# First norm of a two-layer block: turned by chunks of two feature tiles, gain applied as columns, and another order of the first fetches

## What is computed

```python
h = rmsnorm(x, g_mix[l])                 # x * rsqrt(mean(x*x) + eps) * gain, per token
dq, dk, dv, c_q, c_kv_kr, xq, gate_logits = jnp.split(h @ w_in[l], split_idx, axis=-1)
cos_d, sin_d = rotary_tables(positions, DIFF_HEAD_DIM)   # cos, sin of position * inv_freq
cos_r, sin_r = rotary_tables(positions, MLA_ROPE_DIM)
```

## Time and profile before

| | |
|---|---|
| median of 3 runs | 3456.38 us (3451.1 to 3456.73) |
| profiled execution | 3450.06 us |
| its span, first to last instruction | 3448.8 us |
| TensorE (PE) busy | 3329.5 us, 97% |
| VectorE (DVE) busy | 2017.9 us, 59% |
| ScalarE (ACT) busy | 1313.8 us, 38% |
| granted TensorE clock, mean | 0.992 |

### The profile page before, as it was taken

The page is one execution under the profiler, slowest core; times in us unless marked ns, Lnnn a source line. Parts: engine busy times, 40 slices in busy tenths (PEclk is TensorE's granted clock), DMA queues, the critical chain, the costliest instruction groups (busy, mean ns, idle before and its releaser), DMA issues.

```text
span 3448.8 us, 52979 instructions
## 1 busy us (share of the span) xinstructions
PE 3329.5 (97%) x21876; PEld 2720.4 (79%) x21876; DVE 2017.9 (59%) x3798; ACT 1313.8 (38%) x2468; POOL 0.2 (0%) x4
## 2 busy tenths in 40 slices
PE   7989999999999999999999999999999999999998
PEld 6777788888888777788888888777677788788887
DVE  6776753554447776743544448775766578564434
ACT  5466543342225465543332224222443224132222
POOL 0000000000000000000000000000000000000000
PEclk9999999999999999999999999999999999999999
DMA  4221223233333221223333324223311334333332
GB/s 141 80 69 50 56 80 104 86 104 98 98 101 118 90 77 38 59 76 110 98 92 98 98 98 123 81 90 112 114 40 31 108 83 153 122 99 98 98 98 86
DMA packets 353767, 315.11 MB, mean 91 GB/s; under 512 B 10276, under 2 KB 281764, under 8 KB 353528
## 3 DMA queue, kind: packets, MB, share of 16 engines
q1 hardware_dynamic: 352808, 309.56, 29.7%
q10 hardware_dynamic: 720, 2.16, 0.2%
HBM read 288.09 MB, written 23.59 MB: 90 GB/s over the span
## 4 chain that ended last, share of the span: by engine, by line
PE 81%; DVE 11%; ACT 4%; issue 3%; DMA 1%; SPq 0%; DVEq 0%; ACTq 0%
PE banks L532 14%; PE banks L534 13%; PE banks L533 13%; PE banks L427 8%; PE banks L429 8%; PE banks L428 8%; DVE weights_r L368 2%; PE banks L632 1%; PE banks L2877 1%; PE banks L2816 1%; ACT weights_high_r L361 1%; PE banks L1228 1%; PE banks L1241 1%; PE banks L1332 1%; PE banks L2574 1%
## 5 line engine op out<-in xcount | busy, mean ns | idle before, releaser
L368 DVE TENSOR_TENSOR weights_r<-weights,weights_high_r 128x1024 fp32r<-128x1024 f32 (+2 forms) x517 | 593.3, 1155 | 345.8 <-ACT weights_high_r L361 344.7
L532 PE MATMUL banks<-h_T_hi,weights_high_r 128*128 128x512 f32 (+2 forms) x1912 | 760.0, 397 | 9.6 <-DVE h_T_lo L881 3.8
L534 PE MATMUL banks<-h_T_hi,weights_r 128*128 128x512 f32 (+2 forms) x1912 | 737.7, 386 | 0.0
L533 PE MATMUL banks<-h_T_lo,weights_high_r 128*128 128x512 f32 (+2 forms) x1912 | 736.8, 385 | 0.0
L361 ACT ACTIVATE weights_high_r<-weights 128x1024 fp32r<-128x1024 f32 (+2 forms) x517 | 510.6, 998 | 352.0 <-DMA weights<-in_w_mlp 214.0
L532 PEld LDWEIGHTS banks<-h_T_hi,weights_high_r 128*128 128x128 f32 x1912 | 360.8, 189 | 100.3 <-issue 31.4
L534 PEld LDWEIGHTS banks<-h_T_hi,weights_r 128*128 128x128 f32 x1912 | 360.6, 189 | 72.4
L533 PEld LDWEIGHTS banks<-h_T_lo,weights_high_r 128*128 128x128 f32 x1912 | 361.2, 189 | 68.5 <-issue 3.6
L427 PE MATMUL banks<-weights_high_r,h_T_hi 128*128 128x512 f32 (+2 forms) x672 | 278.2, 414 | 3.9 <-DVE weights_r L368 2.1
L429 PE MATMUL banks<-weights_high_r,h_T_lo 128*128 128x512 f32 (+2 forms) x672 | 253.7, 378 | 0.0
L428 PE MATMUL banks<-weights_r,h_T_hi 128*128 128x512 f32 (+2 forms) x672 | 253.3, 377 | 0.0
(11 more groups left out here) (555 smaller groups left out, 5205.6 us busy)
## 6 DMA issues: line engine op xcount, KB each, us to landing
weights<-in_w_in SPq DMA_DIRECT2D x183, 512.0 KB, 3.8
weights<-in_w_mlp SPq DMA_DIRECT2D x128, 512.0 KB, 3.8
weights<-in_ffn_w_in SPq DMA_DIRECT2D x44, 512.0 KB, 3.8
weights<-in_w_out SPq DMA_DIRECT2D x24, 512.0 KB, 3.6
weights<-in_ffn_w_down SPq DMA_DIRECT2D x22, 512.0 KB, 3.6
weights<-in_w_mem_kv SPq DMA_DIRECT2D x16, 512.0 KB, 3.6
weights<-in_w_diff_o SPq DMA_DIRECT2D x16, 512.0 KB, 3.6
weights<-in_w_mla_o SPq DMA_DIRECT2D x8, 512.0 KB, 3.4
```

Source lines behind the costliest of these rows:

```text
L368: ve.e.tensor_tensor(self.part(c.w_raw_r, u), self.part(c.w_raw, u), self.part(c.w_high_r, u).bitcast(F32), ALU.subtract).then_inc(*ve.tel ...
L532: pe.e.matmul(out, lhsT=wh[:, k, :], rhs=hi[k][:, cols], start=(k == 0), stop=False)
L533: pe.e.matmul(out, lhsT=wh[:, k, :], rhs=lo[k][:, cols], start=False, stop=False)
L534: mm = pe.e.matmul(out, lhsT=wl[:, k, :], rhs=hi[k][:, cols], start=False, stop=(k == self.chunks - 1))
```

## The change

StartNorm is rewritten in eight steps. The gain comes as eight columns (one per feature tile) in one small array with the identity, and is applied behind the turning: as the scale of ScalarE's high copy and as the scalar of VectorE's low part. What is turned is x times the inverse root alone (`dve_scale` for tiles 0 and 2, `act_scale` for 1 and 3). A bank now holds two feature tiles of a pair of token tiles (`pe_turn(pair, b)`), each part is made by two instructions of 256 columns, and cq's unit u waits only for chunk b = u (`chunk_ready`). Chunks stand between cq's steps in all three engines' orders, with lags on TensorE for the second pair. The multiplications by g_mix and its fetch are gone from layer 0. On SyncE's queue identity with gain is first, then the six units of weights without a wait for x, then positions and inverse frequencies, vectors and mem. The squares wait for x alone and no longer for the identity. The whole of the tables' VectorE work is now at 7.8 and 7.9, behind all eight chunks' low parts (the last is at 7.7); the sines stay at 11.6. `x_gone` is now: tile 3 squared and tiles 2 and 3 scaled.

```diff
@@ -412,6 +413,8 @@
             part = wh.shape[1]
             if first:
                 pe.wait_ge("low", u)
+                for k in range(part):
+                    pe.wait_all(self.chunk_ready(n, k0[u] + k))
                 if callable(self.ready):
                     for k in range(part):
...
 
-    def tile_scaled(self, t, g, lane):
-        self.c.values[("scaled", self.tag, t, g)] = lane.end
-
     def sp(self):
-        sp = self.c.sp
-        sp.wait_ge("x_in", 1)
         self.c.stream.sp(0)
         for _ in range(self.n):
             yield
 
-    def pe_turn(self, t):
+    def cols(self, pair):
+        return slice(2 * pair * P, 2 * (pair + 1) * P)
+
+    def got(self, pair, b, k):
+        return self.c.slots[(self.tag, pair, b)][:, k * 2 * P:(k + 1) * 2 * P]
+
+    def pe_turn(self, pair, b):
         c, pe = self.c, self.c.pe
-        for g in range(2):
-            pe.wait_ge("scaled", self.tag, t, g)
-            bank = c.fill(self.tag, t, g, ring=self.ring)
-            for k in range(4):
-                at = (4 * g + k) * P
-                mm = pe.e.transpose(bank[:, k * P:(k + 1) * P], self.xg[:, t, at:at + P], c.ident[:, :])
-            mm.then_inc(*pe.tell("filled", self.tag, t, g))
+        for t in (2 * pair, 2 * pair + 1):
+            pe.wait_ge("scaled", self.tag, t, b // 2)
+        bank = c.fill(self.tag, pair, b, ring=self.ring)
+        for k in range(2):
+            at = (2 * b + k) * P
+            for t in range(2):
+                mm = pe.e.transpose(bank[:, (2 * k + t) * P:(2 * k + t + 1) * P], self.xg[:, 2 * pair + t, at:at + P], c.ident[:, :])
+        mm.then_inc(*pe.tell("filled", self.tag, pair, b))
 
     def pe(self):
-        for pair in ((), (), (0, 1), (), (2,), (3,)):
-            for t in pair:
-                self.pe_turn(t)
-            yield
+        self.c.pe.wait_ge("in", "identity")
+        for pair in range(2):
+            for b in range(4):
+                self.pe_turn(pair, b)
+                yield
 
     def act_squares(self, t):
...
         c, ac = self.c, self.c.ac
+        ac.wait_ge("inverse_root", self.roots[t - 1].tag)
         for g in range(2):
-            ac.wait_ge("filled", self.tag, t, g)
-            ac.wait_all(self.free)
-            ac.e.activation(self.tile(c.hT_all[0], t, g), self.got(t, g), ACT.Copy).then_inc(*ac.tell("turned_high", self.tag, t, g))
+            ac.e.activation(self.halves(self.xg[:, t, :])[g], self.halves(c.x[:, t, :])[g], ACT.Copy,
+                            scale=self.sums[0][:, t:t + 1]).then_inc(*ac.tell("scaled_act", self.tag, t, g))
+            c.values[("scaled", self.tag, t, g)] = ac.end
+
+    def act_high(self, pair, b):
+        c, ac = self.c, self.c.ac
+        ac.wait_ge("filled", self.tag, pair, b)
+        ac.wait_all(self.free)
+        for k in range(2):
+            f = 2 * b + k
+            ac.e.activation(c.hT[0][f][:, self.cols(pair)], self.got(pair, b, k), ACT.Copy, scale=c.first_gain[:, f:f + 1]).then_inc(
+                *(ac.tell("turned_high", self.tag, pair, b) if k else ac.step()))
 
     def act(self):
...
-        self.tile_scaled(t, g, ve)
-
-    def dve_low(self, t):
+        self.act_scale(1)
+        self.act_high(0, 0)
+        c.stream.act(2)
+        yield
+        self.act_high(0, 1)
+        self.act_squares(2)
+        c.stream.act(3)
+        yield
+        self.act_high(0, 2)
+        self.act_squares(3)
+        c.stream.act(4)
+        yield
+        self.act_high(0, 3)
+        self.act_scale(3)
+        yield
+        for b in range(4):
+            self.act_high(1, b)
+            yield
+
+    def dve_scale(self, t):
         c, ve = self.c, self.c.ve
         for g in range(2):
-            ve.wait_ge("turned_high", self.tag, t, g)
-            ve.wait_all(self.free)
-            ve.e.tensor_tensor(self.tile(c.hT_all[1], t, g), self.got(t, g), self.tile(c.hT_all[0], t, g).bitcast(F32),
-                               ALU.subtract).then_inc(*ve.frees(self.tag, t, g))
+            ve.e.tensor_scalar(self.halves(self.xg[:, t, :])[g], self.halves(c.x[:, t, :])[g], self.sums[0][:, t:t + 1], None,
+                               ALU.mult).then_inc(*ve.tell("scaled_dve", self.tag, t, g))
+            c.values[("scaled", self.tag, t, g)] = ve.end
+
+    def dve_low(self, pair, b):
+        c, ve = self.c, self.c.ve
+        ve.wait_ge("turned_high", self.tag, pair, b)
+        ve.wait_all(self.free)
+        for k in range(2):
+            f = 2 * b + k
+            ve.e.scalar_tensor_tensor(c.hT[1][f][:, self.cols(pair)], self.got(pair, b, k), c.first_gain[:, f:f + 1],
+                                      c.hT[0][f][:, self.cols(pair)].bitcast(F32), ALU.mult, ALU.subtract).then_inc(
+                *(ve.frees(self.tag, pair, b) if k else ve.step()))
+
+    def dve_root(self, t):
+        ve = self.c.ve
+        for h in range(2):
+            ve.wait_ge("tile_squares", self.tag, t + 1, h)
+        self.roots[t].dve()
+        ve.wait_all(self.x_ready(t, 0))
+        self.dve_scale(t)
 
     def dve(self):
         c, ve = self.c, self.c.ve
-        ve.wait_all(self.gain_in)
-        for t in range(2):
-            for h in range(2):
-                x, gain, xg = (self.halves(y)[h] for y in (c.x[:, t, :], self.gain, self.xg[:, t, :]))
-                ve.wait_all(self.x_ready(t, h))
-                ve.e.tensor_tensor(xg, x, gain, ALU.mult).then_inc(*ve.tell("gained", self.tag, t, h))
-        for h in range(2):
-            ve.wait_ge("tile_squares", self.tag, 1, h)
-        self.roots[0].dve()
-        for g in range(2):
-            self.dve_scale(0, g)
-        yield
+        ve.e.memset(c.stat[:, 0:1], 0.0).then_inc(*ve.tell("zero"))
+        self.dve_root(0)
         c.stream.dve(1)
-        yield
-        for t in range(2):
-            self.dve_low(t)
-        c.stream.dve(3)
-        yield
-        for h in range(2):
-            ve.wait_ge("tile_squares", self.tag, NT - 1, h)
-        self.roots[2].dve()
-        for t in range(2, NT):
-            for g in range(2):
-                x, gain, xg = (self.halves(y)[g] for y in (c.x[:, t, :], self.gain, self.xg[:, t, :]))
-                ve.wait_all(self.x_ready(t, g))
-                ve.e.scalar_tensor_tensor(xg, x, self.sums[0][:, t:t + 1], gain, ALU.mult, ALU.mult).then_inc(*ve.tell("gained", self.tag, t, g))
-                self.tile_scaled(t, g, ve)
-        yield
-        for t in range(2, NT):
-            self.dve_low(t)
-            yield
+        self.dve_low(0, 0)
+        yield
+        for b in range(1, 4):
+            c.stream.dve(b + 1)
+            self.dve_low(0, b)
+            if b == 3:
+                self.dve_root(2)
+            yield
+        for b in range(4):
+            self.dve_low(1, b)
+            yield
+
+    def chunk_done(self, pair, k):
+        return [("emptied", self.tag, pair, k // 2)]
+
+    def done(self, t=None):
+        return [("emptied", self.tag, pair, b) for pair in (range(2) if t is None else (t // 2,)) for b in range(4)]
+
+    def x_gone(self):
+        return [("tile_squares", self.tag, NT - 1, 1), ("scaled", self.tag, NT - 1, 1), ("scaled", self.tag, NT - 2, 1)]
 
 
...
         c, ve, t_ = self.t.c, self.t.c.ve, self.t
-        ve.e.memset(c.stat[:, 0:1], 0.0).then_inc(*ve.tell("zero"))
         ve.wait_all(t_.ready)
...
         if l == 0:
             tables = Tables(c, ((self.cos_d, self.sin_d), (self.cos_r, self.sin_r)), [("in", "positions")])
-            P_.at(Load(c, "identity", [(c.ident[:, :], i["identity"])], []), (-2.9,))
+            P_.at(Load(c, "identity", [(c.ident_gain, i["identity_gain"])], []), (-2.9,))
             P_.at(Load(c, "positions", [(c.pos_i[:, :], i["positions"]),
-                                        (tables.freq, i["inv_freq"][0, :].partition_broadcast(P))], [], True), (-3,))
+                                        (tables.freq, i["inv_freq"][0, :].partition_broadcast(P))], [], True), (0.5,))
         norm_cells = wide_norm_cells(c)
-        gain_load = Load(c, tag("g_mix"), [(norm_cells[0], i["g_mix"][l].partition_broadcast(P))], hT_free if l else [])
-        P_.at(gain_load, (norm_times[0][0] - 1,))
+        if l:
+            gain_load = Load(c, tag("g_mix"), [(norm_cells[0], i["g_mix"][l].partition_broadcast(P))], hT_free)
...
         normed, x_gone = norm.done(), norm.x_gone()
 
-        def section(name, dst, col, n, free, ring="gemm 2"):
...
 
 
         cq, ckv = plain(X[0:4]), plain(X[4:8])
-        cq_job, ckv_job = section("cq", cq, C_CQ, MQ, x_gone), section("ckv", ckv, C_CKV, MKV + MR, x_gone)
+        cq_job, ckv_job = section("cq", cq, C_CQ, MQ, x_gone, **({} if l else {"chunk_ready": norm.chunk_done})), section("ckv", ckv, C_CKV, MKV + MR, x_gone)
         P_.products(cq_job, ckv_job)
         if l == 0:
-            P_.at(tables.whole, (-1.5,))
-            P_.at(tables.rest, (6.2,))
+            P_.at(tables.whole, (7.8,))
+            P_.at(tables.rest, (7.9,))
```

(66 more changed lines are left out.)

10 lines of the change are left out of this document (2 added, 8 removed).

## The result

The changed kernel takes 3511.83 us (median of 5 runs, 3509.13 to 3516.62) against 3456.38 (3451.1 to 3459.89): a ratio of 1.0164, 95% interval 1.0152 to 1.0176. It is 55 us slower; the prediction had 3458.5 and a range to 3465.

A forecast was written before the change was run, and what follows sets the result against it. TensorE was taken as the bound, 81% of the chain; ckv's delay 0.95, tile 3's copy 0.2 and clock 2.0 summed to +3.1 us: 3453.2 from the profiled execution, stated as 3458.5 near the median; range 3449 to 3465.

The forecast's parts named there:

- Other edits: all priced 0: Start: smaller or later identity, positions, frequencies and vectors, dropped g_mix fetch and SyncE waits together cost 0 us.
- behind the start nothing is changed: Rest of the kernel: a start change is worth only what it moves TensorE's continuous work forward, no more.
- Tile 1 of x: Start: lands at 6.4 us beside six units of weights, bounds 6.2 and 8.2.
- an even split of the bytes: Start fetches: at about 200 GB/s per queue, tile 1 of x would come 0.6 us later, the sum 0.6 us longer.
- First pass: cq's first pass: from first product at 13.8 us, with TensorE slow until 15.6, it ends at 24.4 us.
- Wait for bank 0: Before cq's second pass: TensorE idles 1.8 us until ScalarE's copy out of tile 0 ends at 28.1 us.
- Clock behind the long idle: After the 6.8 us TensorE gap before ckv: restart at a lower clock costs 2.0 us, between 0 and 3.8.
- the tables eat the gain: Before ckv: tables end at 42.9 us, delaying sines and copy out; ckv at 44.6 instead of 37.8; 78%.
- (a): Before ckv: sines finish before TensorE needs bank 0, ckv starts at 37.8; -5.8 us, 3450.6; chance 12%.
- (b): Start: weights' transfers delay tile 1 of x to 11 us instead of 6.4; +7.7 us, 3464; chance 7%.
- (c): TensorE's gap before ckv: the clock does not fall; +1.1 us, 3457.5; inside the forecast's range, no separate chance.
- (d): Start: the first product isn't earlier, so the tables come later still; 3463 us or more; chance 3%.

The follow-up runs named there:

- e1: Changed kernel with the identity-and-gain tile allocated last instead of third, nothing else different: 3460.33 us, ratio 1.0014 to the kernel before.
- e2: Kernel before with 8 unused columns (32 bytes per partition) behind the identity, moving all later tiles up 32 bytes: 3505.7 us, ratio 1.0150.
- e10: Changed kernel, identity and gain allocated last, SyncE again waiting for tile 1 of x before fetching weights: 3455.89 us, one run, beside 3456.73 for the kernel before.
- e7: Changed kernel, identity and gain allocated last, tables' first part moved earlier and sines behind the copies out of cq's tiles 2 and 3: 3457.64 us, ratio 1.0007.
- e13: As e7, but with the sines later still (19.2 and 20.2) and the first layer's Gains at 24 to 27 instead of 15 to 18: 3458.19 us, ratio 1.0008.
- e5: Kernel before with 8 unused columns ahead of the weights and 24 behind: weights 32 bytes higher, all others 128 bytes higher: 3512.53 us, ratio 1.0165.
- e12: Kernel before with 24 unused columns (96 bytes) behind the identity: 3516.27 us, ratio 1.0173.

## Why the prediction was wrong

**The step that failed is "Other edits: all priced 0", together with "behind the start nothing is changed".** Among the edits I listed identity, positions and a dropped fetch by their transfers, and did not ask what eight more columns in a tile in the third place do to all tiles behind it. Its price: e1 takes it out of the change (51.5 us less), e2 puts it alone into the kernel before (1.0150, 51 us more). 10872 matmuls with 5.2 ns each are 56.5 us of busy time; that the time grew by some 5 us less would fit some of them lying where TensorE does not set the pace, which no run tells apart. What happens inside TensorE or SBUF is not shown either; the runs show that the place is the cause, not why. The trace of before could not have given this number, as all parts of its products are in place; but the edit could have been named as unpriced, and a row could have shown the stakes: at a step of 0.227 us, one percent of it is 25 us.

The Trainium skill ("SBUF — State Buffer", Operand start alignment) says that an operand must start at a multiple of its element size and adds that this is "about legality, not speed". All places tried here are multiples of 32 bytes and all work, so the runs agree as far as they go; on speed they add what the page leaves open.

**The rest, by its own steps,** each against the profile of after or of e1:

- Tile 1 of x at 7.0 us, not 6.4. e10 gives the price of sharing, 1.0 us. That the queues interleave, as the Trainium skill ("DMA: Bandwidth & Descriptors", Issuing engines are not separate DMA queues) says, is so in the trace: both moved data between 4.4 and 7.0 us. My sum for an even split of the bytes gave just this 7.0, but by luck: x's queue moved 0.72 of the 1.09 MB there, 277 GB/s, which is the share that I had preferred. What I had missed is that by 7.0 us it had moved 1.26 MB, more than the 1.05 of tiles 0 and 1: part of tile 2 went beside tile 1.
- First transpose 11.29 us (10.7 predicted), first product 14.31 (13.8). The chunk's parts took 0.84 and 0.88 us, predicted 0.86 from rows. What I cited for them from the Trainium skill ("VectorE: DVE Perf Modes", The TRN2 errata — SBUF-src ops pay a fixed extra latency per instruction) is said of operands in SBUF, while these parts read PSUM; no run here tests it.
- First pass: predicted to 24.4, measured until 26.2. Mis-sized term: the slow pace at the start lasted until 19.8 us, 8.5 us after the first transpose, where I gave it 5. In e1 it ended at 18.1.
- Wait for bank 0: 1.95 us (1.8 predicted), put down to the copy out, as said.
- The second pass has a term that I lacked: in the profile of after the granted clock fell as that short wait ended. The windows of after, then of e1 (columns as in rows 7):

```profile
32.00:33.00 1.00, 1.00 (x5) 1.00 (x4) 0.00 (x0) 0.00 (x0) 0.00 (x0) 0.50 0.00 0
46.00:47.00 1.00, 0.00 (x0) 0.00 (x0) 0.33 (x2) 1.00 (x5) 0.00 (x0) 0.50 0.00 0
48.00:49.00 1.00, 1.00 (x6) 1.00 (x6) 0.90 (x3) 0.98 (x2) 0.00 (x0) 0.50 0.00 0
51.00:52.00 1.00, 1.00 (x10) 1.00 (x9) 0.97 (x6) 1.00 (x4) 0.00 (x0) 1.00 0.00 0
```

```profile
32.00:33.00 1.00, 1.00 (x7) 1.00 (x7) 0.27 (x1) 0.70 (x2) 0.00 (x0) 1.00 0.51 74
```

  At 0.50, the 1.2 GHz level, after makes 5 matmuls where e1, behind the same wait of 1.96 us, makes 7. This gives 1.6 of the 2.45 us by which ckv starts later in after (47.39) than in e1 (44.94); the other 0.9 is the longer slow pace at the start. In the traces of e7 and e13 the clock fell behind the same wait (1.95 and 1.96 us), in e10 it did not. What decides it is open.
- Tables 38.50 to 45.72, 7.2 us as predicted; in e1 36.05 to 43.27 (35.7 to 42.9 predicted) and ckv at 44.94 (44.6 predicted); idle 6.38 us in both (6.8 predicted).
- Clock behind the long idle: it fell, both in after and e1. The step was 0.24 us in 288-column matmuls instead of 0.132, for 12 to 15 of them: 1.3 to 1.6 us, where I took 2.0. The start's price that I went by was itself read too high: four, not some six, of the first products in the kernel before started 0.30 us or more apart.

The sum for the start was +3.1 us; e1 has +2.4 by the first matmul behind ckv (60.83 against 58.42) and 1.0014 (1.0003 to 1.0024) by the time, 5 us, with 1 and 8 as ends. This part, that the tables eat the gain, held; e7 shows it directly, since the idle goes when tables and sines are moved. That 3460.33 us of e1 lies near the forecast of 3458.5 is in part luck, as a late first transpose and a longer slow pace stand against a cheaper clock. Of the rivals (a) failed, and (b), (c) and (d) did not happen. The slower outcome came from a mechanism that stood in no case.

## What to carry to other kernels

A change in the size of one on-chip tile moves all tiles allocated behind it: round each up to 128 bytes per partition, or allocate odd-sized ones last, and look at the pace of steady matmuls before anything else when a local edit has a global effect. A busy time that grows at an equal count of instructions is such an effect, and here neither the waits nor the chain's shares (PE 81% and 82%) gave it away; the mean ns of one form did. Check too where a tile really begins: four columns more moved these tiles by 32 bytes, not by 16. When work is moved out of a stall, list what stands behind its new place in each engine's order: here sines behind the tables held a copy out, and that a bank.

## What was not expected of the hardware

Matmuls in fp32r with 512 columns and a weight load each start every 0.227 to 0.228 us if both operands begin at multiples of 128 bytes per partition, and every 0.233 to 0.234 us if one of them begins 32 or 96 bytes behind such a multiple; at 64 bytes a moving operand costs less (0.230), a stationary one the same (0.233). With 384 columns it is less: line 533 takes 335 ns before, 336 in e2, 338 in e5 and 339 in e12. 128 bytes cost nothing (ratio 1.0000, 0.9988 to 1.0012). VectorE and ScalarE did not feel it: their busy times are 2017.7 and 1313.4 us with 32 bytes in e2, 2017.9 and 1313.8 without. Why 64 bytes are cheap for the moving operand alone, why 96 bytes came out 10 us above 32, what less than 32 bytes costs, and whether two operands off by the same distance pay at all, is open.
